# Causal mask of the scores: two VectorE additions in the accumulators in place of four TensorE products per pair of heads

## The chip, the cores and the metric

One core of a Trainium2 chip runs the whole program. The metric is the device time of one execution in microseconds (us); 1 us is 1000 ns. Engines are called PE (TensorE, its weight loads PEld), DVE (VectorE), ACT (ScalarE), POOL (GpSimd) and SP (SyncE, which here issues the loads of the weights).

## The reference, cut to what matters

Two stacks of layers run over 256 tokens of width 1024, all in float32. The first has two layers; the second has four, each made of a feed-forward part, a mixer and another feed-forward part. The four mixers are stick-breaking, block ("moba"), latent ("mla") and again stick-breaking attention, with 16 heads each. The change touches the block and the latent mixer. For 256 tokens there is one block, so block attention is plain causal attention:

```python
l_own = jnp.einsum('bhqd,bhkd->bhqk', qc, k_own).astype(jnp.float32) * scale
l_own = jnp.where(opos[None, :] <= cpos[:, None], l_own, NEG)
p = jax.nn.softmax(jnp.concatenate([l_sel, l_own], axis=-1), axis=-1)
...
logits = jnp.where(kpos[None, :] <= qpos[:, None], logits, NEG)   # latent attention
p = jax.nn.softmax(logits, axis=-1).astype(v.dtype)
```

NEG is -1e30.

## The kernel before, in words

Nearly all time goes into products with weights, which come from memory as a stream of chunks of 128 x 2048 float32 (a ring of 6). Each chunk is split in two parts: ScalarE writes the high part (`split_hi`, L204), VectorE the rest (`split_lo`, L211), in rings of 3, and TensorE makes three products of each pair of tiles (high x high, high x low, low x high). `chunk_used` tells that a chunk's parts may be overwritten.

Each engine runs one instruction stream in order, written out by hand, and the streams meet only through semaphores (`sig` names an event, `when` waits for it). There is no planner at run time; the order of the work between the attention's operations is fixed by the tables `PLAN` (block) and `LAT_STEPS` (latent): each step p of the loop over the 8 pairs of heads has three parts of other work ("feed": products of the projections that later pairs need, and early products of the output projection).

The accumulator memory has two tensors of four banks, `acc` and `tb`. Banks 0 and 1 of `tb` take the scores of the two heads of a pair: columns 0 to 127 are queries 0 to 127 against keys 0 to 127, columns 128 to 383 are queries 128 to 255 against all keys. So the parts that need a triangular mask are columns 0 to 127 and 256 to 383. Banks 2 and 3 take the transposed probabilities.

In step p, with the line numbers of the profile:

- TensorE (`softmax_pe`): waits for the exponentials of pair p-1 (`exps`), because the scores overwrite the banks that ScalarE read; makes the scores, L1161 (128 x 128) and L1163 (128 x 256), two of each; adds the mask with four products of the bf16 identity and the bf16 mask (L1166, L1167) and signals `scores`. In block attention L1161 and L1163 use 64 rows of the array, in latent attention 128. Then it waits for `weights` of pair p-1 and transposes them (L1177), runs two parts of feed, multiplies the transposed probabilities with the values (L870, L873, `heads_out`), and runs the third part of feed.
- VectorE (`softmax_dve`): waits for `scores`; takes the maximum over the columns, L1224 (128 x 256) and L1225 (128 x 512), scales it, L1227, and signals `top`; does its feed of part 0; waits for `exps`; takes the reciprocal of the sums, L1231, multiplies the probabilities, L1234 and L1235, and signals `weights`; does its feed of parts 1 and 2. Its feed is the splits L211 and, in block attention, the rotation of the positions (L1086, L1087, L1089, event `turned`, which waits for TensorE's L1021), in latent attention the taking of the queries (L1540).
- ScalarE (`softmax_act`): copies the transposed probabilities of pair p-1 to memory (L1198 in block, L1201 in latent attention); waits for `top`; makes the exponentials, L1207 and L1209, two of each with a row that reads the sum, and signals `exps`; then its feed: in block attention the copy L1071 (event `copied`, for which TensorE's rotation L1021 waits) and the splits L204, in latent attention L1521, L1531 and L204.

After every second pair L879 (ScalarE) and L883 (VectorE) take the heads' output. The mask is a constant `cst[:, C_CAUSNEG:...]`, 128 x 128 float32 with -1e30 above the diagonal; at the start of the program VectorE casts it to bf16 (L2311) for L1166 and L1167.

Of the kernel before, what the change touches and what calls it, by code (L numbers as in the profile page):

```python
# [21 lines left out]
P = 128  # L22
SEQ, D = 256, 1024
# [19 lines left out]
CAUSAL = P + SEQ  # L43
# [12 lines left out]
C_ROT, C_FOLD, C_TRI, C_ALL, C_STRICT, C_CAUSNEG, C_STRNEG = [P + 1 + i * P for i in range(7)]  # L56
# [5 lines left out]
class Signals:  # L62
# [14 lines left out]
    def sig(self, name, key, by=1):  # L77
        sem = self.sem(name)
        self.count[name] += by
        assert (name, key) not in self.marks, (name, key)  # L80
        self.marks[name, key] = self.count[name]
        return sem, by

    def when(self, name, key):
        return self.sem(name), 1 if self.known is None else self.known[name, key]
# [18 lines left out]
def write(nc, known, stream, x, pT, positions, gains, gains_T, lam_qk, lru_cols, gates, consts, out):  # L104
    f32, f32r, bf16 = mybir.dt.float32, mybir.dt.float32r, mybir.dt.bfloat16
    ALU, ACT, AX = mybir.AluOpType, mybir.ActivationFunctionType, mybir.AxisListType
# [3 lines left out]
    with ctx:  # L110
        def sb(name, shape, dt=f32):
            return ctx.enter_context(nc.sbuf_tensor(name, shape, dt))

        S = Signals(known, lambda name: ctx.enter_context(nc.semaphore(name)))
        sig, when = S.sig, S.when
# [13 lines left out]
        cst = sb("cst", [P, C_END])  # L129
# [7 lines left out]
        tb = ctx.enter_context(nc.psum_tensor("tb", [P, 4, 512], f32))  # L137
# [3 lines left out]
        ident_b, causal_b, strict_b = bfc[:, 0, :], bfc[:, 1, :], bfc[:, 2, :]  # L141
# [720 lines left out]
        def heads_out(pe, i, m, v, w):  # L862

            g, at = m // 2, SEQ * (m % 2)
            if m % 2 == 0 and g >= 2:
                pe.wait_ge(*when("cat_lo", (i, g - 2)))
            o = [acc[HD * u:HD * u + HD, head_bank(g), at:at + SEQ] for u in range(2)]
            for u in range(2):
                hd = 2 * m + u
                pe.matmul(o[u], v[:, 0, hd * HD:(hd + 1) * HD], w(u)[:, 0:SEQ], start=True, stop=True)  # L870
            for u in range(2):
                hd = 2 * m + u
                last = pe.matmul(o[u][:, P:SEQ], v[:, 1, hd * HD:(hd + 1) * HD], w(u)[:, SEQ:CAUSAL], start=False,  # L873
                                 stop=True, skip_group_check=True)
            last.then_inc(*sig("head_out", (i, m)))
# [278 lines left out]
        def softmax_pe(pe, i, c_out, n, q, k, v, p_T, feed, qk_ready, v_ready):  # L1154
            for p in range(N_PAIRS + 1):
                if p < N_PAIRS:
                    qk_ready(p)
                    if p:
                        pe.wait_ge(*when("exps", (i, p - 1)))
                    for u in range(2):  # L1160
                        pe.matmul(tb[:, u, 0:P], q(2 * p + u)[:, 0:P], k(2 * p + u)[:, 0:P], start=True, stop=True)  # L1161
                    for u in range(2):
                        pe.matmul(tb[:, u, P:CAUSAL], q(2 * p + u)[:, P:SEQ], k(2 * p + u), start=False, stop=True,  # L1163
                                  skip_group_check=True)
                    for u in range(2):
                        pe.matmul(tb[:, u, 0:P], ident_b, causal_b, start=False, stop=True, skip_group_check=True)  # L1166
                        last = pe.matmul(tb[:, u, 2 * P:3 * P], ident_b, causal_b, start=False, stop=True,  # L1167
                                         skip_group_check=True)
                    last.then_inc(*sig("scores", (i, p)))
                if p >= 1:  # L1170
                    m = p - 1
                    pe.wait_ge(*when("weights", (i, m)))
                    if m:
                        pe.wait_ge(*when("flip_out", (i, m - 1)))
                    for u in range(2):
                        for j in range(3):
                            last = pe.transpose(tb[:, 2 + u, j * P:(j + 1) * P],  # L1177
                                                probs[:, 2 * (m % 2) + u, j * P:(j + 1) * P], ident)
                    last.then_inc(*sig("flipped", (i, m)))
                feed.some(p, 0)  # L1180
                feed.some(p, 1)
                if p >= 1:
                    m = p - 1
                    pe.wait_ge(*when("flip_out", (i, m)))
                    v_ready(m)
                    heads_out(pe, i, m, v, lambda u: p_T(m, u))
                feed.some(p, 2)
            out_rest(pe, i, c_out, n)
# [30 lines left out]
        def softmax_dve(dve, i, scale, behind):  # L1219
            for p in range(N_PAIRS + 1):  # L1220
                if p < N_PAIRS:
                    pair = slice(2 * p, 2 * p + 2)
                    dve.wait_ge(*when("scores", (i, p)))
                    dve.tensor_reduce(mx[:, pair, 0], tb[:, 0:2, 0:P], AX.X, ALU.max)  # L1224
                    dve.tensor_reduce(mx[:, pair, 1], tb[:, 0:2, P:CAUSAL], AX.X, ALU.max).then_inc(*sig("own", ("mx", i, p)))  # L1225
                    dve.wait_ge(*when("own", ("mx", i, p)))
                    dve.tensor_scalar(nmx[:, pair, :], mx[:, pair, :], -scale, None, ALU.mult).then_inc(*sig("top", (i, p)))  # L1227
                behind(p, 0)
                if p < N_PAIRS:
                    dve.wait_ge(*when("exps", (i, p)))  # L1230
                    dve.reciprocal(rs[:, pair, :], sm[:, pair, :]).then_inc(*sig("own", ("rs", i, p)))  # L1231
                    dve.wait_ge(*when("own", ("rs", i, p)))
                    pr = probs[:, 2 * (p % 2):2 * (p % 2) + 2, :]
                    dve.tensor_tensor(pr[:, :, 0:P], pr[:, :, 0:P], rs[:, pair, 0:1].to_broadcast([P, 2, P]), ALU.mult)  # L1234
                    dve.tensor_tensor(pr[:, :, P:CAUSAL], pr[:, :, P:CAUSAL], rs[:, pair, 1:2].to_broadcast([P, 2, SEQ]),  # L1235
                                      ALU.mult).then_inc(*sig("weights", (i, p)))
                behind(p, 1)
                behind(p, 2)
                if p >= 2 and p % 2 == 0:
                    cat_lo(dve, i, p // 2 - 1)  # L1240
# [195 lines left out]
        class LatFeed(Feed):  # L1436
# [24 lines left out]
            def q(self, unit, p):  # L1461
                pe, i = self.pe, self.i
                if p == 0:
                    pe.wait_ge(*when("q_lo", (i, 1)))
                for u in range(2):
                    o = lat_bank(unit)[:, u * SEQ:(u + 1) * SEQ]
                    for kt in range(3):
                        at_ = 3 * (2 * p + u) + kt
                        k, a = self.c + UP_Q[at_ // Q_BLOCKS], P * (at_ % Q_BLOCKS)
                        if (u, kt) == (0, 0) or at_ % Q_BLOCKS == 0:  # L1470
                            pe.wait_ge(lo_done, k + 1)
                        hi, lo = w_hi[:, k % SPLIT, a:a + P], w_lo[:, k % SPLIT, a:a + P]
                        pe.matmul(o, hi, q_T[:, kt, 0, :], start=kt == 0, stop=False)
                        pe.matmul(o, hi, q_T[:, kt, 1, :], start=False, stop=False)
                        last = pe.matmul(o, lo, q_T[:, kt, 0, :], start=False, stop=kt == 2)
                        if at_ % Q_BLOCKS == Q_BLOCKS - 1:
                            last.then_inc(chunk_used, 1)
                if p < HEADS // 2 - 1:
                    last.then_inc(*sig("pair_done", (i, p)))

            def k(self, unit, g, b):
                pe, k = self.pe, self.c + UP_KV[g]
                pe.wait_ge(lo_done, k + 1)
                if (g, b) == (0, 0):
                    pe.wait_ge(*when("kv_lo", (self.i, 1)))
                s = k % SPLIT
                for f in range(2):
                    o = lat_bank(unit)[:, f * SEQ:(f + 1) * SEQ]
                    for kt in range(2):
                        a = kt * D + (2 * b + f) * P  # L1490
                        hi, lo = w_hi[:, s, a:a + P], w_lo[:, s, a:a + P]
                        pe.matmul(o, hi, kv_T[:, kt, 0, :], start=kt == 0, stop=False)
                        pe.matmul(o, hi, kv_T[:, kt, 1, :], start=False, stop=False)
                        last = pe.matmul(o, lo, kv_T[:, kt, 0, :], start=False, stop=kt == 1)
                last.then_inc(*sig("k_done", (self.i, g, b)))
# [1005 lines left out]
```

## Time and profile before

| | |
|---|---|
| median of 3 runs | 2611.5 us (2610.76 to 2611.63) |
| the profiled execution | 2610.73 us, span 2608.9 us |
| busy: PE, PEld, DVE, ACT, POOL | 2572.1, 2228.0, 1674.5, 1380.8, 61.1 us |
| mean granted clock of TensorE | 0.998 |
| chain that ended last, by engine | PE 92%, DVE 4%, ACT 3%, issue 1% |
| L1166 and L1167 | 32 instructions each |
| L1224, L1225, L1227 | 16 instructions each |

The span runs from the first to the last instruction of the profiled execution; the time includes what lies around it. A busy share says how long an engine worked, not whether somebody waited for it. The chain of waits is followed back from the last instruction: at each step to what released it. The block attention's loop lies at about 1343 to 1430 us of the span, the latent one's at 1853 to 1910 us. The starts of matmuls are recorded and their ends are modelled, so two matmuls in a row overlap in the rows; their pace is read from the starts.

### The profile page before, as it was taken

How to read it: one execution, taken by the hardware profiler on the slowest of the kernel's cores; microseconds unless marked ns; L12 is line 12 of the kernel's file. 1: busy time of each engine (PE TensorE's matmuls, PEld its weight loads, DVE VectorE, ACT ScalarE, POOL GpSimd, SP SyncE). 2: the span in 40 equal slices, each digit the busy share in tenths (PEclk: the TensorE clock that was granted, in tenths of full speed). 3: DMA queues.
4: the chain of work that ended last, by engine and by line, in shares of the span. 5: the costliest groups of instructions: out<-in, count | busy, mean ns of one | idle time of the engine just before them, and what ended most of it. 6: DMA issues, size and time to landing. Idle time of an engine off the chain costs nothing.

```text
span 2608.9 us, 38082 instructions
## 1 busy us (share of the span) xinstructions
PE 2572.1 (99%) x14854; PEld 2228.0 (85%) x14854; DVE 1674.5 (64%) x1827; ACT 1380.8 (53%) x1640; POOL 61.1 (2%) x30
## 2 busy tenths in 40 slices
PE   8999999999999999999999999999999999999998
PEld 7888898888888988888888888888888888898887
DVE  7766687556765666666666666666766666665665
ACT  6644565445545664454455544544654454465544
POOL 0000000001000000000000000000000000000000
PEclk9999999999999999999999999999999999999999
DMA  7455534554554345555543455454345555543551
GB/s 272 144 196 191 181 138 178 193 191 173 196 192 178 130 148 191 193 177 193 193 146 117 176 192 193 178 193 177 130 154 193 185 185 186 186 161 114 194 193 65
DMA packets 63496, 454.36 MB, mean 174 GB/s; under 512 B 7088, under 2 KB 7344, under 8 KB 8992
## 3 DMA queue, kind: packets, MB, share of 16 engines
q1 hardware_dynamic: 62064, 449.15, 48.0%
q0 software_dynamic: 896, 3.05, 0.4%
q8 instruction: 78, 1.28, 0.2%
q10 hardware_dynamic: 432, 0.68, 0.1%
q14 instruction: 26, 0.21, 0.0%
HBM read 451.79 MB, written 1.05 MB: 174 GB/s over the span
## 4 chain that ended last, share of the span: by engine, by line
PE 92%; DVE 4%; ACT 3%; issue 1%; DMA 0%; ACTq 0%; DVEq 0%
PE tb L489 28%; PE tb L494 14%; PE acc L287 10%; PE acc L288 10%; PE acc L289 10%; PE acc L253 2%; PE acc L255 2%; PE acc L256 2%; PE acc L897 1%; DVE w_lo L211 1%; PE acc L489 1%; PE acc L899 1%; PE acc L898 1%; PE tb L318 1%; ACT w_hi L204 1%
## 5 line engine op out<-in xcount | busy, mean ns | idle before, releaser
L211 DVE TENSOR_TENSOR w_lo<-raw,w_hi 128x2048 fp32r<-128x2048 f32 x416 | 952.6, 2293 | 314.7 <-ACT w_hi L204 314.5
L204 ACT ACTIVATE w_hi<-raw 128x2048 fp32r<-128x2048 f32 x425 | 812.9, 1914 | 314.4 <-PE acc L289 276.5
L489 PE MATMUL tb<-xT,w_hi 128*128 128x512 f32 x3168 | 792.0, 392 | 0.0
L489 PEld LDWEIGHTS tb<-xT,w_hi 128*128 128x128 f32 x3168 | 576.3, 188 | 108.5 <-DVE big L682 0.2
L494 PEld LDWEIGHTS tb<-xT,w_lo 128*128 128x128 f32 x3168 | 432.1, 190 | 31.0
L494 PE MATMUL tb<-xT,w_lo 128*128 128x256 f32 x3168 | 441.7, 282 | 0.0
L287 PE MATMUL acc<-w_hi,cat 128*128 128x512 f32 x1024 | 402.8, 393 | 3.5 <-DVE cat L582 3.5
L288 PE MATMUL acc<-w_hi,cat 128*128 128x512 f32 x1024 | 399.9, 390 | 0.0
L289 PE MATMUL acc<-w_lo,cat 128*128 128x512 f32 x1024 | 398.7, 389 | 0.0
L287 PEld LDWEIGHTS acc<-w_hi,cat 128*128 128x128 f32 x1024 | 192.7, 188 | 42.8 <-DVE cat L582 3.9
L289 PEld LDWEIGHTS acc<-w_lo,cat 128*128 128x128 f32 x1024 | 192.3, 188 | 41.1
L288 PEld LDWEIGHTS acc<-w_hi,cat 128*128 128x128 f32 x1024 | 192.8, 188 | 34.9
L629 ACT ACTIVATE big<-tb 128x512 f32<-128x512 f32 x80 | 47.7, 596 | 263.7 <-PE tb L494 263.7
L253 PE MATMUL acc<-xT,w_hi 128*128 128x256 f32 x560 | 167.1, 298 | 1.6 <-DVE big L1089 0.8
L639 ACT ACTIVATE big<-tb 128x512 f32<-128x512 f32 x88 | 52.7, 599 | 213.2 <-PE tb L494 213.2
L255 PE MATMUL acc<-xT,w_hi 128*128 128x256 f32 x560 | 158.2, 283 | 0.0
L256 PE MATMUL acc<-xT,w_lo 128*128 128x256 f32 x560 | 158.1, 282 | 0.0
L671 DVE TENSOR_TENSOR big<-tb,big 128x512 f32<-128x512 f32 x80 | 55.3, 691 | 142.6 <-ACT big L629 142.6
L682 DVE TENSOR_TENSOR big<-tb,big 128x512 f32<-128x512 f32 x88 | 60.8, 691 | 113.7 <-ACT big L639 113.7
L253 PEld LDWEIGHTS acc<-xT,w_hi 128*128 128x128 f32 x560 | 106.9, 191 | 7.4 <-issue 3.0
L255 PEld LDWEIGHTS acc<-xT,w_hi 128*128 128x128 f32 x560 | 107.1, 191 | 2.3 <-issue 2.2
L256 PEld LDWEIGHTS acc<-xT,w_lo 128*128 128x128 f32 x560 | 107.0, 191 | 0.0
(349 smaller groups left out, 2882.7 us busy)
## 6 DMA issues: line engine op xcount, KB each, us to landing
raw<-in_stream SPq DMA_DIRECT2D x425, 1024.0 KB, 4.8
h<-in_x SPq DMA_DIRECT2D x2, 512.0 KB, 5.9
xn<-in_gates POOLq DMA_DIRECT2D x2, 512.0 KB, 8.0
gain<-in_gains POOLq DMA_DIRECT2D x2, 512.0 KB, 5.3
out<-xn SPq DMA_DIRECT2D x2, 512.0 KB, 2.9
cst<-in_consts SPq DMA_DIRECT2D x1, 832.0 KB, 12.6
raw<-in_stream ACTq DMA_DIRECT2D x1, 512.0 KB, 8.3
raw<-in_stream SPq DMA_DIRECT2D x1, 512.0 KB, 9.1
```

What stands on the lines that cost most here:

```text
L204: act.activation(w_hi[:, k % SPLIT, :], raw[:, k % RAW, :], ACT.Copy).then_inc(hi_done, 1)
L211: dve.tensor_tensor(w_lo[:, k % SPLIT, :], raw[:, k % RAW, :], w_hi[:, k % SPLIT, :], ALU.subtract).then_inc(lo_done, 1)
L253: pe.matmul(dst(f), hi, src[:, kt, 0, :], start=kt == 0 and (after is None or f == 0), stop=False, skip_group_check=after is not None)
L255: pe.matmul(dst(f), hi, src[:, kt, 1, :], start=False, stop=False, skip_group_check=after is not None)
L256: last = pe.matmul(dst(f), lo, src[:, kt, 0, :], start=False, stop=kt == kts - 1, skip_group_check=after is not None)
L287: pe.matmul(dst(t, nn), a_hi, b_hi, start=start and kt == 0, stop=False)
L288: pe.matmul(dst(t, nn), a_lo, b_hi, start=False, stop=False)
L289: last = pe.matmul(dst(t, nn), a_hi, b_lo, start=False, stop=stop and kt == kts - 1)
L489: return pe.matmul(bank, w_hi[:, c % SPLIT, at:at + P], xT[:, kt, :, :].rearrange("p a t -> p (a t)"), start=first, stop=last)
L494: return pe.matmul(bank[:, 0:SEQ], w_lo[:, c % SPLIT, at:at + P], xT[:, kt, 0, :], start=False, stop=last)
L671: dve.tensor_tensor(two(f_sum), up_part(k or None, 0, 0), two(f_bg), ALU.add).then_inc(hid_p, 1)
L682: dve.tensor_tensor(two(f_up), up_part(k, 1, 0), two(f_bu), ALU.add).then_inc(hid_v, 1)
```

## The change

TensorE no longer adds the mask: the four products per step are gone, and `scores` is signalled by the second L1163. VectorE adds the float32 constant instead, in place in the accumulators, once for columns 0 to 127 and once for columns 256 to 383 of both heads (128 x 256 elements each), and waits for the second addition before the maxima. Nothing else is changed: the casts of the constants at the start stay.

```diff
@@ softmax_pe
                     for u in range(2):
-                        pe.matmul(tb[:, u, P:CAUSAL], q(2 * p + u)[:, P:SEQ], k(2 * p + u), start=False, stop=True,
-                                  skip_group_check=True)
-                    for u in range(2):
-                        pe.matmul(tb[:, u, 0:P], ident_b, causal_b, start=False, stop=True, skip_group_check=True)
-                        last = pe.matmul(tb[:, u, 2 * P:3 * P], ident_b, causal_b, start=False, stop=True,
+                        last = pe.matmul(tb[:, u, P:CAUSAL], q(2 * p + u)[:, P:SEQ], k(2 * p + u), start=False, stop=True,
                                          skip_group_check=True)
                     last.then_inc(*sig("scores", (i, p)))
@@ softmax_dve
                     dve.wait_ge(*when("scores", (i, p)))
+                    mask = cst[:, C_CAUSNEG:C_CAUSNEG + P].unsqueeze(1).to_broadcast([P, 2, P])
+                    dve.tensor_tensor(tb[:, 0:2, 0:P], tb[:, 0:2, 0:P], mask, ALU.add).then_inc(*sig("own", ("m0", i, p)))
+                    dve.tensor_tensor(tb[:, 0:2, 2 * P:CAUSAL], tb[:, 0:2, 2 * P:CAUSAL], mask,
+                                      ALU.add).then_inc(*sig("own", ("m1", i, p)))
+                    dve.wait_ge(*when("own", ("m1", i, p)))
                     dve.tensor_reduce(mx[:, pair, 0], tb[:, 0:2, 0:P], AX.X, ALU.max)
```

## Rows read from the trace of the kernel before

**Rows 1.** Windows: length, busy us (instructions) by engine, granted clock, DMA.

```profile
0.00:20.00 20.00, 9.31 (x48) 8.56 (x49) 7.38 (x11) 9.80 (x13) 2.10 (x8) 0.91 0.92 335
1343.00:1430.00 87.00, 83.74 (x651) 71.47 (x650) 55.42 (x80) 45.85 (x98) 0.00 (x0) 1.00 0.38 134
1853.00:1910.00 57.00, 55.62 (x400) 46.70 (x400) 38.87 (x66) 34.18 (x94) 0.00 (x0) 1.00 0.36 130
```

**Rows 2.** Chain of waits, block attention: start us, us, engine and line.

```profile
1346.80 0.61 DVE small L1225
...
1393.57 0.66 PE tb L1177 x6
...
1419.13 0.81 ACT big L1198
...
1425.96 0.61 DVE small L1225
```

**Rows 3.** Chain of waits, latent attention.

```profile
1856.85 0.61 DVE small L1225
...
1864.46 0.61 DVE small L1225
```

**Rows 4.** TensorE's waits, block attention: total us, times, longest.

```profile
PE acc L1021 <- ACT big L1071: 1.5, 2, 0.8
...
PE tb L1161 <- DVE big L1089: 0.8, 1, 0.8
PE tb L1177 <- DVE xn L1235: 0.2, 1, 0.2
```

**Rows 5.** Timeline, TensorE, block step 0: start, length, instruction, idle before.

```profile
1343.35 0.38 PE L1163 MATMUL tb<-big 64*128 64x256 f32 x2
...
1343.66 0.10 PEld L1166 LDWEIGHTS tb<-bfc 128*128 128x128 bf16 x1 [0.33 <-issue]
1343.66 0.23 PE L1166 MATMUL tb<-bfc 128*128 128x128 bf16 x1
...
1343.84 0.22 PE L1167 MATMUL tb<-bfc 128*128 128x128 bf16 x1
```

**Rows 6.** VectorE's groups by form: busy us, mean ns, idle before.

```profile
L1688 DVE TENSOR_TENSOR ropeA<-tb,cst 128x256 f32<-128x256 f32 x1 | 0.4, 424 | 3.5 <-PE tb L1567 3.5
```

**Rows 7.** Timeline, VectorE, block step 0.

```profile
1349.39 0.18 DVE L1231 RECIPROCAL small<-small 128x4 f32<-128x4 f32 x1 [1.79 <-ACT xn L1209]
1349.60 0.42 DVE L1234 TENSOR_TENSOR xn<-xn,small 128x256 f32<-128x256 f32 x1
1349.94 0.68 DVE L1235 TENSOR_TENSOR xn<-xn,small 128x512 f32<-128x512 f32 x1
```

**Rows 8.** TensorE's waits, latent attention.

```profile
PE tb L1161 <- DVE big L1540: 1.2, 1, 1.2
PE tb L1161 <- ACT xn L1209: 0.5, 1, 0.5
```

**Rows 9.** Timeline, latent steps 2, 4, 5 and 7.

```profile
1870.02 0.17 DVE L1227 TENSOR_SCALAR small<-small 128x4 f32<-128x4 f32 x1
1870.39 0.37 ACT L1207 ACTIVATE xn<-tb,small 128x128 f32<-128x128 f32 x1
...
1887.22 0.21 ACT L1209 ACTIVATION_READ_ACCUMULATOR xn<-tb,small 128x1 f32 x1
...
1887.58 0.68 PE L1161 MATMUL tb<-big 128*128 128x128 f32 x4
...
1893.18 0.21 ACT L1209 ACTIVATION_READ_ACCUMULATOR xn<-tb,small 128x1 f32 x1
...
1893.73 0.71 PE L1161 MATMUL tb<-big 128*128 128x128 f32 x4
...
1905.42 0.68 DVE L1235 TENSOR_TENSOR xn<-xn,small 128x512 f32<-128x512 f32 x1
...
1906.48 0.82 PE L1177 MATMUL tb<-cst,xn 128*128 128x128 f32 x6
```

## The prediction

> **What bounds the kernel now.** Over the whole run TensorE is busy nearly all the time, so a change that takes work from it looks like a gain. The question is what holds in the two stretches that the diff touches, the attention of block kind (1343 to 1430 us) and the latent one (1853 to 1910 us), each of 8 steps (pairs 0 to 7). First read the busy time there: TensorE 83.74 of 87.00 us and 55.62 of 57.00 us, VectorE 55.42 and 38.87 us [rows 1]. By shares TensorE is full and VectorE has a third free. Shares say nothing about order, so next comes the chain of waits. In the block stretch it does not stay on TensorE: it passes through the score maximum L1225 on VectorE in steps 0, 1, 2, 3, 5 and 7 (six such rows, the first and the last shown), and only in steps 4 and 6 through TensorE and the copy L1198 [rows 2]. In the latent stretch it passes L1225 in steps 0 and 1 and then is TensorE's [rows 3]. What closes the loop is this: maximum, then the exponentials on ScalarE, then on the same in-order ScalarE the copy L1071 and the split L204, then VectorE's split L211 and turn L1086 to L1089, and behind them in VectorE's queue the maximum of the next step. TensorE's waits show the same: it waits twice for L1071 (1.5 us), once for L1089 (0.8 us) and at the end for the weights L1235 [rows 4]. So a delay put ahead of the maximum is not swallowed by VectorE's idle third; it travels round this loop, once per step.
>
> **What is removed.** Per step four bf16 products (L1166, L1167). They start at 1343.66 us, the last at 1343.84 us, so 0.06 us apart: 4 x 0.055 = 0.22 us of TensorE per step, 3.5 us for 16 steps [rows 5]. In front of them stands an idle 0.33 us put down to "issue" [rows 5]. It would make the saving 0.5 us per step if the mask caused it; I count nothing of it, since the product ahead of them, L1163, uses 64 rows of the array and the next one 128 [rows 5], and that stays so after the removal. The Trainium skill (TensorEngine Tiling, Key Properties) says that changing the tiling mode drains TensorE, which is this case; without that rule the block stretch would gain up to 8 x 0.33 = 2.6 us more. No run so far shows the mask gone, so that is open, and it is a bound. In this trace 0.22 us of TensorE helps only where TensorE sets the pace.
>
> **What is added.** Per step two additions of 128x256 in the accumulators and a wait for the second, ahead of the two maxima. No row has VectorE writing an accumulator. The nearest is L1688, the same shape and sources (accumulator and constants, written to SBUF): 424 ns [rows 6]. Two such instructions in a row start 0.34 us apart (L1234 at 1349.60, L1235 at 1349.94), and after a wait on its own result the engine goes on 0.03 us after the end (L1231 ends at 1349.57) [rows 7]. So D = 0.34 + 0.42 + 0.04 = 0.80 us per step. The low end is 0.68 us (two starts 0.34 apart, the wait free), the high end 0.92 us (no overlap at all); below zero is excluded, since nothing goes away on VectorE. I take 0.80, from the row of the same shape. The Trainium skill (VectorE: DVE Perf Modes, the TRN2 errata) has 120 + FD cycles at 0.96 GHz with an accumulator source, by estimate 0.39 us for 256 elements, and D would be 0.77. Queued behind the wait on VectorE are the maxima and then the splits; ScalarE's exponentials wait for them, and TensorE waits for those, since the scores of step p+1 overwrite the banks that they read. No DMA is added or moved, and the cast that makes the bf16 mask stays.
>
> **The sum, block stretch.** Six steps have the maximum on the chain: 6 x 0.80 = +4.8 us. In step 4 the chain is TensorE's (L1177 at 1393.57) [rows 2], the delay of 0.80 is hidden under a product that ScalarE waits for anyway, and TensorE's saving is half felt: -0.1. In step 6 VectorE stood waiting for the scores and the exponentials behind the copy L1198 of 0.81 us [rows 2]; the scores come some 0.3 us sooner and about 0.1 is taken out of the wait for the copy, so +0.4. The last link, L1177 at the weights, waits already (0.2 us) [rows 4]. Together +5.1 us. TensorE's savings in the six steps go into longer waits.
>
> **The sum, latent stretch.** Steps 0 and 1 are on the chain: TensorE waits already 0.5 us for the exponentials [rows 8], so +1.6 us when step 2 begins. Then VectorE and ScalarE have slack, and it is used up: each step makes them later by 0.8 less what they used to wait for TensorE (in step 2 the maxima were ready at 1870.02 + 0.17 and the exponentials began at 1870.39, 0.2 us; 0.1 to 0.3 us in these steps) [rows 9], so 2.1 after step 2, 2.7 after step 3, 3.5 after step 4, while TensorE, 0.22 sooner each step, is late by only 0.9. The exponentials of step 4 end at 1887.22 + 0.21 = 1887.43 and TensorE's next scores start at 1887.58 [rows 9]: with 0.1 us between them TensorE takes over nearly all, +3.5. Step 5: exponentials late by 4.3, they ended 1893.39, the scores start at 1893.73 [rows 9], 0.3 us of slack: +4.0. In step 7 the mask starts when the scores come, so the weights L1235 are late by 4.0 - 0.2 + 0.8 = 4.6; they ended at 1906.10 and L1177 started at 1906.48 [rows 9], slack 0.4: +4.2 us. Behind it nothing waits for anything that isn't late by the same.
>
> Together 5.1 + 4.2 = +9.3 us. The profiled execution took 2610.73 us and becomes 2620.0; the median of the runs, 2611.5, lies 0.8 above it, so I forecast 2620.8. Counted as above, 15 of the 16 steps carry D in full, so D of 0.68 gives +7.5 and of 0.92 gives +11.1 (9.3 less and plus 15 x 0.12); the slacks and the savings may be off by 2 us together. The forecast's own range is 2616.7 to 2625.
>
> **Rivals.** First, no loss, the other side: at the gate where TensorE waits for L1071 and for the exponentials, the loop through VectorE and ScalarE has slack that the chain does not show, and TensorE sets the pace. Then 3.5 us are saved, 2608.0. For it speak the 83.74 of 87.00 us [rows 1]; against it the six L1225 on the chain. It decides at D: hidden if the slack per step were over 0.80 us, and 0.1 and 0.3 us are what the rows give [rows 9]. Chance 0.06. Second, half: in the latent stretch ScalarE and VectorE make up their delay and only the block stretch pays: 5.1 - 8 x 0.22 = +3.3, 2614.8; for it, the chain there is TensorE's after step 1. Chance 0.07. Third, faster: the 0.33 us in front of L1166 goes too and TensorE sets the pace, 16 x 0.55 = 8.8, 2602.7; chance 0.01. Fourth, the clock: granted clock is 1.00 in both stretches [rows 1], the longest wait of TensorE in them is 1.2 us [rows 8], and I forecast one of about 2.6 us in latent step 4. In the first 20 us, with longer pauses, it was 0.91, which is 3.6 us at 1.2 GHz, costing 1.8 us of work [rows 1]. One or two such stretches would give 2622.6 or 2624.4. The Trainium skill (TensorE: Matmul & The Clock Gate, Part 1) has the clock halved after an idle stretch of TensorE. Chance 0.05, and it lies within the range. The last 0.81 is the forecast.
>
> **The numbers.** A measurement of this kernel can tell about 0.2% (5.2 us) from no change, so slower is over 2616.7. Slower: 0.81 + 0.05 = 0.86, less 0.02 for a forecast that falls short; same: 0.06 + 0.07 + 0.02 = 0.15; faster 0.01. The range reaches down to 2614.5, into the second rival, and up to 2625.5 for a large D or the clock.
>
> **What would show it.** Two new VectorE groups of 16, each 0.42 us; L1225 to start about 0.8 us further behind the scores. Waits of TensorE for L1071 four or more times instead of two, and over 6 us; in the latent stretch waits of L1161 for L1209 of some 5 us instead of 0.5. Busy time of TensorE down by some 3 us and the span up by 9. If the block stretch is not longer by about 5 us and the latent one by about 4, the sum is wrong; if the additions last under 0.3 us or over 0.6, D is; if the total is unchanged, the loop is not what bounds.

## The result and the profile after

The changed kernel takes 2622.19 us (median of 5 runs, 2621.85 to 2623.84), the kernel before 2611.02 us beside it: a ratio of 1.0042, 95% interval 1.0031 to 1.0053, 11.2 us slower. Forecast were 2620.8 us and a range of 2614.5 to 2625.5. Measured again beside each other (e12), the same two kernels gave 2622.63 and 2612.06 us, a ratio of 1.0040 (1.0027 to 1.0054).

The page of the changed kernel hardly differs from the one before. Busy time and the chain by engine:

```profile
PE 2571.3 (98%) x14790; PEld 2226.9 (85%) x14790; DVE 1686.4 (64%) x1859; ACT 1380.2 (53%) x1640; POOL 61.1 (2%) x30
...
PE 90%; DVE 5%; ACT 3%; issue 1%; DMA 0%; ACTq 0%; DVEq 0%
```

TensorE has 64 products fewer but only 0.8 us less of busy time (their modelled lengths overlap their neighbours, and a fall of the clock, below, lengthened others), VectorE has 11.9 us more. Neither says where the 11 us are. The groups of VectorE by form do say what was added (busy us, mean ns, idle before):

```profile
L1221 DVE TENSOR_TENSOR tb<-tb,cst 128x256 f32<-128x256 f32 x16 | 6.8, 425 | 1.3 <-PE tb L1163 1.2
L1225 DVE TENSOR_REDUCE small<-tb 128x2 f32<-128x256 f32 x16 | 6.8, 424 | 0.5
L1222 DVE TENSOR_TENSOR tb<-tb,cst 128x256 f32<-128x256 f32 x16 | 6.7, 422 | 0.0
```

L1221 and L1222 are the additions, 425 and 422 ns beside the 424 ns of [rows 6]: adding in place in the accumulators takes as long as the addition of that row, which writes to SBUF. Timeline of VectorE in block step 0:

```profile
1347.02 0.42 DVE L1221 TENSOR_TENSOR tb<-tb,cst 128x256 f32<-128x256 f32 x1
1347.35 0.42 DVE L1222 TENSOR_TENSOR tb<-tb,cst 128x256 f32<-128x256 f32 x1
1347.80 0.42 DVE L1225 TENSOR_REDUCE small<-tb 128x2 f32<-128x256 f32 x1
```

From the first addition to the first maximum it is 0.78 us, forecast 0.80. TensorE's waits (total us, times, longest), first in the block stretch (1342 to 1450 us), then in the latent one (1855 to 1920 us):

```profile
PE acc L1021 <- ACT big L1071: 7.3, 4, 2.0
PE tb L1173 <- DVE xn L1236: 1.7, 1, 1.7
PE tb L1161 <- DVE big L1089: 0.8, 1, 0.8
```

```profile
PE tb L1161 <- ACT xn L1205: 5.1, 4, 2.7
PE tb L1161 <- DVE big L1541: 1.2, 1, 1.2
PE tb L1173 <- DVE xn L1236: 0.3, 1, 0.3
```

The wait for the copy L1071 went from 1.5 us in two places [rows 4] to 7.3 us in four (6.3 us in e7, whose clock does not fall), the one for the weights of the last pair (L1173 on L1236, before L1177 on L1235) from 0.2 us to 1.7, the one for the exponentials (L1205 is L1209 of before) from 0.5 [rows 8] to 5.1 us. That is where the time is. In the chain of waits of the latent stretch the second maximum now appears seven times, where it appeared twice [rows 3]:

```profile
1864.73 0.61 DVE small L1226
...
1873.14 0.61 DVE small L1226
...
1878.70 0.61 DVE small L1226
...
1885.29 0.61 DVE small L1226
...
1895.40 0.61 DVE small L1226
...
1902.14 0.61 DVE small L1226
...
1913.55 0.61 DVE small L1226
```

**The same in lengths.** The two stretches can be cut out of any profile: from the start of the first L1161 of the attention to the start of the next L318 (the transposes for the next layer). They repeat within 0.1 us between profiles as long as the clock stays, far closer than the totals, which drift by 1 to 2 us between executions. "Falls" counts how often the granted clock went to half in the stretch.

```
profile                      block (falls)  latent (falls)
before                       101.20 (0)     64.78 (0)
changed                      107.79 (1)     68.97 (0)
changed again (e12)          108.81 (2)     69.03 (0)
e1 splits held, VectorE      101.54 (0)     65.23 (0)
e2 splits held, TensorE       99.60 (0)     63.87 (0)
e3 changed, filled waits     106.24 (0)     69.43 (1)
e4 one addition              108.36 (2)     68.54 (0)
e5 no mask                   100.82 (0)     63.80 (0)
e6 mask by both              106.63 (0)     70.19 (1)
e7 block alone changed       106.21 (0)     64.76 (0)
e8 latent alone changed      101.17 (0)     69.38 (1)
e9 additions twice           115.70 (2)     75.09 (1)
e10 e2, one split more        98.92 (0)     63.86 (0)
e11 mixed                     98.38 (0)     63.15 (0)
```

Step by step, the delay of the scores of pair p (start of its first L1161, changed less before, each stretch counted from its own pair 0):

```
pair      1     2     3     4     5     6     7
block   0.79  1.59  1.40  3.68  3.51  5.43  5.24
latent  0.57  1.59  1.35  1.12  3.42  4.02  3.92
```

Call a gate a place where TensorE waits for L1071 or for the exponentials. At each gate it takes over all that VectorE and ScalarE are late (0.79, 1.59, then 3.2); between the gates it gains back 0.2 us per step, the removed products. The 3.68 at block pair 4 and the 5.43 at pair 6 hold a part that the additions do not explain, the fall of the clock: in e7, without a fall, they are 3.16 and 3.84. Busy time and granted clock by the microsecond around it (the column behind the five engines is the clock):

```profile
1387.00:1388.00 1.00, 0.00 (x0) 0.00 (x0) 0.00 (x0) 1.00 (x5) 0.00 (x0) 1.00 0.00 0
1388.00:1389.00 1.00, 0.99 (x3) 0.58 (x3) 0.00 (x0) 1.00 (x1) 0.00 (x0) 0.80 0.00 0
1389.00:1390.00 1.00, 1.00 (x5) 0.67 (x4) 0.22 (x1) 0.75 (x1) 0.00 (x0) 0.50 0.00 0
...
1391.00:1392.00 1.00, 1.00 (x7) 1.00 (x6) 1.00 (x2) 0.00 (x0) 0.00 (x0) 0.50 0.00 0
1392.00:1393.00 1.00, 1.00 (x9) 0.82 (x10) 0.97 (x4) 0.00 (x0) 0.00 (x0) 1.00 0.00 0
```

```profile
1388.01 1.53 PE L1021 MATMUL acc<-big,cst 128*128 128x512 f32 x2 [1.93 <-ACT big L1071]
...
1390.19 0.41 PE L998 MATMUL acc<-w_hi,xT 128*128 128x256 f32 x1
1390.40 0.41 PE L999 MATMUL acc<-w_lo,xT 128*128 128x256 f32 x1
```

TensorE stood idle for 1.93 us (timeline, second fence), and from about 1388.6 to 1392 us it ran at 1.2 GHz: a product every 0.21 us instead of every 0.12. Without a fall the stretch is 106.2 us (e3 and e7), so the fall cost 1.55 us.

### The profile page after: what moved, and what is told of

Same layout as the page of the kernel before. It is cut to its first block, busy times and chain, and to the rows that moved or that the text cites. A ratio compares the mean times of both kernels' runs of the same rounds, so it can differ in the third digit from the quotient of the medians.

```text
span 2620.0 us, 37986 instructions
## 1 busy us (share of the span) xinstructions
PE 2571.3 (98%) x14790; PEld 2226.9 (85%) x14790; DVE 1686.4 (64%) x1859; ACT 1380.2 (53%) x1640; POOL 61.1 (2%) x30
## 3 DMA queue, kind: packets, MB, share of 16 engines
HBM read 451.79 MB, written 1.05 MB: 173 GB/s over the span
## 4 chain that ended last, share of the span: by engine, by line
PE 90%; DVE 5%; ACT 3%; issue 1%; DMA 0%; ACTq 0%; DVEq 0%
PE tb L489 27%; PE tb L494 14%; PE acc L287 10%; PE acc L288 10%; PE acc L289 10%; PE acc L253 2%; PE acc L255 2%; PE acc L256 2%; DVE w_lo L211 1%; PE acc L897 1%; PE acc L489 1%; PE tb L318 1%; PE acc L899 1%; PE acc L898 1%; PE acc L997 1%
## 5 line engine op out<-in xcount | busy, mean ns | idle before, releaser
L211 DVE TENSOR_TENSOR w_lo<-raw,w_hi 128x2048 fp32r<-128x2048 f32 x416 | 952.5, 2292 | 315.3 <-ACT w_hi L204 315.1
```

Source lines behind the costliest of these rows:

```text
L211: dve.tensor_tensor(w_lo[:, k % SPLIT, :], raw[:, k % RAW, :], w_hi[:, k % SPLIT, :], ALU.subtract).then_inc(lo_done, 1)
```

## The experiments

Theory: the additions lie on a loop through VectorE's and ScalarE's in-order queues that had almost no slack, so their 0.8 us is paid in nearly every step. Rivals: the additions cost time by themselves (VectorE in the accumulators); or TensorE's products set the pace; or the clock makes the difference.

### Each half of the change (e5, e6), each stage (e7, e8)

**e5** takes the four products out of the kernel before and puts nothing in their place; it leaves out the causal mask of both mixers:

```diff
-                        pe.matmul(tb[:, u, 0:P], ident_b, causal_b, start=False, stop=True, skip_group_check=True)
-                        last = pe.matmul(tb[:, u, 2 * P:3 * P], ident_b, causal_b, start=False, stop=True,
```

> The kernel before without the four mask products and without any mask: leaves out the causal mask of block and latent attention. Loop theory: TensorE's 0.22 us per step count only where TensorE sets the pace, block steps 4 and 6 and latent steps 2 to 7, so 1.8 us less than before (2609.2), the removed 0.33 us in front of L1166 reappears in front of the next product. Rival, TensorE sets the pace everywhere: 3.5 us less (2607.5); with the 0.33 us gone too, 6 to 8.8 us less.

Measured 2611.15 against 2612.45 us, ratio 0.9996 (0.9987 to 1.0005): 1.3 us less. The interval of the total reaches from 3.4 us less to 1.3 more and decides little. The lengths do: block 0.38 us shorter, latent 0.98, together 1.4 us, near the 1.8 of the loop theory and far from the 3.5 that the products occupy. And the idle 0.33 us is still there, now in front of the next product (timeline of the weight loads):

```profile
1343.28 0.31 PEld L1163 LDWEIGHTS tb<-big 64*128 64x128 f32 x4
1343.92 0.19 PEld L253 LDWEIGHTS acc<-xT,w_hi 128*128 128x128 f32 x1 [0.33 <-issue]
```

In the kernel before it stood in front of L1166 in the 8 block steps (L1166's idle time "issue: 2.7, 8") and in none of the 8 latent ones, where L1163 uses 128 rows as well. So it belongs to the step from 64 to 128 rows of the array, not to the mask; the Trainium skill's sentence on tiling modes (TensorEngine Tiling, Key Properties) agrees.

**e6** leaves the products in and puts the additions behind them.

> Mask added twice, by TensorE's products and by VectorE's additions (the sum of both masks the same entries out). Loop theory: the whole cost of the changed kernel and about 1 us more, the saving of TensorE's products being felt in some five steps: 2622 to 2624. Rival, the removal is worth its full 3.5 us: 2625.7.

Measured 2621.92 against 2612.45 us, ratio 1.0038 (1.0024 to 1.0052): 9.5 us, not the 11 or 12 that I had expected. In its profile the block stretch has no fall of the clock; whether that holds for the other four executions is not known. The block stretch is 106.63 us, only 0.4 us longer than with the products gone (106.24, e3). In the latent stretch it is 70.19 us, 1.2 over the changed kernel, and a fall of the clock is mixed in; with some 0.4 us for it, as in e8, an estimate of 0.8 us is left for the products. So almost all of the cost is the additions', and the removal gives back about 1.2 us of it.

**e7 and e8** make the change under `if i == 1` (block) or `if i == 2` (latent) alone.

> The change in block attention alone, latent attention as before. Loop theory: +5.1 us, and +1.5 where the clock falls, so 2616 to 2618. Rival (only the stretch with TensorE's own waits pays): the whole 11 us here.

> The change in latent attention alone, block attention as before. Loop theory: +4.2 us, 2615.2, with TensorE waiting 5 us for the exponentials; perhaps 1.5 us more where the clock falls behind the idle 2.7 us of step 4. Rival (slack of VectorE and ScalarE there swallows it): under +1 us.

Measured 2618.39 and 2616.98 against 2612.45 us: ratios 1.0023 (1.0014 to 1.0032) and 1.0019 (1.0009 to 1.0028). The stretch that was changed is 5.0 us longer in e7 and 4.6 in e8 (with a fall of about 0.4 us; 4.2 in the changed kernel), the other is as before to 0.03 us. The two costs add up and do not touch each other. In both profiles the clock also fell once at 441 us, in a feed-forward stage that the change does not touch. TensorE waits there 1.8 us for VectorE's L582 (e7's waits; 1.7 us in the kernel before, whose clock stayed up), so the place is not made by the change. In e10, with the mask on TensorE throughout, the clock falls at 131 us. Falls are not the change's alone.

### The length of the additions (e4, e9)

**e4** makes one addition of 128x512 over both parts; **e9** makes the pair twice.

```diff
-                    mask = cst[:, C_CAUSNEG:C_CAUSNEG + P].unsqueeze(1).to_broadcast([P, 2, P])
-                    dve.tensor_tensor(tb[:, 0:2, 0:P], tb[:, 0:2, 0:P], mask, ALU.add).then_inc(*sig("own", ("m0", i, p)))
-                    dve.tensor_tensor(tb[:, 0:2, 2 * P:CAUSAL], tb[:, 0:2, 2 * P:CAUSAL], mask,
-                                      ALU.add).then_inc(*sig("own", ("m1", i, p)))
+                    mask = cst[:, C_CAUSNEG:C_CAUSNEG + P].unsqueeze(1).unsqueeze(1).to_broadcast([P, 2, 2, P])
+                    own_ = tb[:, 0:2, 0:CAUSAL].rearrange("p u (b k) -> p u b k", k=P)[:, :, 0:3:2, :]
+                    dve.tensor_tensor(own_, own_, mask, ALU.add).then_inc(*sig("own", ("m1", i, p)))
```

> The changed kernel with one addition of 128x512 over both masked parts in place of two of 128x256. Loop theory: D goes from 0.80 to 0.69 + 0.04 = 0.73 us, 15 steps carry it in full, so 1.0 us less than the changed kernel (2621.2), within 0.3. Rival, a fixed cost per addition of more than the 0.08 us seen: over 2 us less.

> The changed kernel with the two additions and their wait made twice per step (the mask added twice, the same entries out). Loop theory: D goes from 0.80 to 1.60 us and every slack is used up already, so 15 to 16 steps carry 0.80 more: 12 to 13 us over the changed kernel, 6 to 6.5 of it in the block stretch (first scores to the transposes behind it, without falls of the clock 112.4 us instead of 106.2) and 5.6 to 6.4 in the latent one (74.8 instead of 69.0). Rival, part of the 9.2 us is not carried by the length of the additions (a one-time effect of VectorE writing the accumulators): less than 10 us more.

e4: 2622.77 against 2612.62 us, 1.0038 (1.0024 to 1.0051), in its total not to be told from the changed kernel, where 1.0 us less was forecast. The addition lasts 693 ns. The latent stretch is 0.43 us shorter for 7 steps of 0.06 us less, so the rival of a large fixed cost per addition is out; in the block stretch the clock fell twice. e9: 2638.48 against 2612.06 us, 1.0104 (1.0088 to 1.0119). The latent stretch is 6.1 us longer than the changed kernel's, with a fall; the block one is 9.5 us over the 106.2 without falls, and of these some 2.6 are its two falls, by estimate (e12 has two as well and is 2.6 us over 106.2, but one of e9's lies elsewhere, at the very end of the stretch). That leaves about 6.9 and 5.7 to 6.1 us for 8 steps of 0.8 each: the cost goes with the length of what stands on the loop. The total is 15.9 us over the changed kernel where 12 to 13 were forecast; three falls in the profiled execution, of which the changed kernel has one or two, account for a part.

### Slack put into the loop (e1, e2, e10)

In the order of before, VectorE's last work ahead of a maximum is often a split L211 of 2.3 us for a chunk that TensorE needs only much later. Here these splits are put in a list and issued behind the next maximum (main lines; the one of block step 6 stays where it was):

```diff
+                if part == 0:
+                    while hold:
+                        split_lo(dve, c, hold.pop(0))
...
-                        split_lo(dve, c, unit[1] + SPLIT)
+                        if hold is None:
+                            split_lo(dve, c, unit[1] + SPLIT)
+                        else:
+                            hold.append(unit[1] + SPLIT)
```

> The kernel before (mask on TensorE) with the same splits held back. Loop theory: it loses the 3.3 us of waits that TensorE has in the block stretch and 0.5 us in the latent one, so 2607 to 2609, and the additions' version in the same order is up to 3.5 us (16 x 0.22) faster than this, not slower. Rival, TensorE's products alone set the time: same as before, 2611.

> The changed kernel, with the splits L211 that stood between VectorE's feed and the next maximum held back until after that maximum (block and latent steps). Loop theory: the 0.80 us per step were paid because VectorE's queue (split, turn, maximum) and ScalarE's formed a loop with no slack; with some 2.3 us of slack per step the two additions are hidden, TensorE's waits for L1071 and for the exponentials nearly vanish, and the time is some 3 to 6 us below the kernel before (2605 to 2608). Rival, the additions cost by themselves (accumulators shared with TensorE, or the handshake): the time stays 9 us or more above the same order with the mask on TensorE.

e2 (mask on TensorE): 2609.62 against 2612.62 us, 0.9989 (0.9980 to 0.9998). e1 (mask on VectorE): 2612.77 against 2612.62, 1.0002 (0.9993 to 1.0011), where 2605 to 2608 was forecast. In this order the additions cost 1.94 us in the block stretch and 1.36 in the latent one, 3.3 us where they cost 9.2 before. The rival that they cost by themselves is out, since the same instructions cost a third when only the order around them is different. But my expectation that they would be hidden entirely was wrong. TensorE's waits in e1's block stretch:

```profile
PE tb L1177 <- DVE xn L1240: 1.7, 1, 1.7
PE acc L1021 <- ACT big L1071: 1.4, 2, 1.1
PE acc L253 <- DVE big L1089: 0.8, 1, 0.8
PE tb L1165 <- DVE big L1089: 0.7, 1, 0.7
PE acc L253 <- DVE w_lo L211: 0.6, 1, 0.6
```

and in e2's:

```profile
PE acc L253 <- DVE big L1089: 0.8, 1, 0.8
PE tb L1181 <- DVE xn L1239: 0.5, 1, 0.5
PE acc L1021 <- ACT big L1071: 0.5, 1, 0.5
PE tb L1165 <- DVE big L1089: 0.3, 1, 0.3
```

The weights of the last pair are waited for 1.7 us instead of 0.5: TensorE is through with the feed of step 7 before they come. Comparing the two profiles pair by pair, TensorE comes later with the mask on VectorE in block steps 0, 1, 3, 5 and 7 and latent steps 0, 5 and 7, and 0.2 us sooner in block 2, 4 and 6 and latent 1 to 4. **e10** is e2 with the split of block step 6 held back too.

> Mask on TensorE, splits held back as in e2, and also the split of block step 6, which stood ahead of the maximum of step 7. Loop theory: TensorE's wait of 0.5 us for the last weights goes, block stretch 99.1 us instead of 99.6, latent 63.9, 0.5 us less than e2. Rival, the split then delays the weights of step 7 by its own 2.3 us: block stretch 100 or more.

2608.84 against 2612.06 us, 0.9988 (0.9979 to 0.9997); block stretch 98.92 us, the wait of 0.5 us gone.

### A mix of both (e11)

```diff
+        BY_VECTOR = {(1, 2), (1, 4), (1, 6), (2, 1), (2, 2), (2, 3)}
```

The pairs (mixer, step) in this set take the mask by VectorE, the others by TensorE, on top of e10.

> As e10, with the mask on VectorE in the steps where e1 showed TensorE not later but 0.2 us sooner (block steps 2, 4, 6, latent steps 1, 2, 3) and on TensorE in the other ten. Loop theory: the additions are hidden there and each step gives 0.2 us: block stretch 0.5 to 0.6 us and latent 0.5 to 0.6 us shorter than e10, the shortest of all. Rival, any delay of VectorE travels on whatever the slack: longer than e10.

2607.69 against 2612.06 us, 0.9983 (0.9974 to 0.9992): faster than the kernel before by 4.4 us, and the stretches 98.38 and 63.15 us are the shortest of all, 0.54 and 0.71 below e10. Its waits in the block stretch are e10's to the digit, so the six pairs of additions are hidden. Between e10 and e11 the total's intervals overlap; the lengths tell them apart.

### The clock (e3, e12)

**e3** is the changed kernel with 16 products by a tile of zeros, added to a sum already under way, ahead of the wait for L1071 in block steps 0, 1, 3 and 5. The zeros take the place of the bf16 mask, so the first two layers' differential attention runs without its causal mask.

```diff
+                if e in (3, 4, 7, 10):
+                    for _ in range(16):
+                        self.pe.matmul(fed_bank(e + 1)[:, 0:P], causal_b, ident_b, start=False, stop=False,
+                                       skip_group_check=True)
```

> The changed kernel, with 16 products by a tile of zeros (0.055 us each, 0.9 us) ahead of four waits for L1071 in the block steps 0, 1, 3 and 5, where TensorE stands idle anyway. Clock theory: 1.5 of the 11 us come from one fall of the granted clock to 0.50 behind the idle 1.93 us of step 3; with 1.0 us of idle left the clock stays at 1.00 in the block stretch and the time is 1 to 2 us below the changed kernel (2620.5). Rival, the fall comes by itself whatever TensorE does, or the idle time is not free: same as the changed kernel (2622) or above.

> The changed kernel again beside the others on the same chip. Loop theory: block stretch 106.2 us plus 1.5 for each fall of the clock in it, latent 69.0 plus up to 0.5 for a fall; total 9 to 12 us over before, the profiled time explained by the count of falls. Rival, the falls belong to the block step 3 wait as such: one there again.

e3: 2621.94 against 2612.62 us, 1.0036 (1.0022 to 1.0050). In the block stretch the clock stays at 1.00 and the length is 106.24 us: the filling costs nothing (e7, without it, has 106.21), and no fall comes. Its waits there:

```profile
PE acc L1025 <- ACT big L1075: 2.7, 3, 1.0
PE tb L1177 <- DVE xn L1240: 1.7, 1, 1.7
```

But in its profile the clock fell in the latent stretch, which isn't filled, and once at 130 us, and the total did not come out 1 to 2 us lower: 9.3 us over before where the changed kernel has 10.6 to 11.2, which the intervals do not separate. e12, the changed kernel once more: 2622.63 against 2612.06 us. This time the clock fell twice in the block stretch, behind the waits of steps 0 and 3 (windows around both):

```profile
1349.50:1353.00 3.50, 2.10 (x4) 1.07 (x5) 1.53 (x4) 3.15 (x7) 0.00 (x0) 0.73 0.48 199
1387.00:1391.00 4.00, 2.45 (x6) 1.42 (x7) 0.68 (x1) 3.29 (x8) 0.00 (x0) 0.71 0.00 0
```

The two cost 2.6 us, less than twice 1.55, and the next wait for L1071, at step 1, is 1.05 us instead of 1.7: it took a part of the first fall's delay. The length of the wait alone does not decide whether the clock falls: there is no fall at step 3 in e7, which has the same wait of 1.9 us, and none in the changed kernel behind the 2.65 us at latent step 4, where e3, e6 and e8 have one. That filling the waits prevents falls is consistent with e3's block stretch; with one profile it is not shown, since e6 and e7 have none there either.

## Why the prediction was right

- **What bounds the stretches.** The chain's passing through L1225 was read as a loop with no slack. Shown: e7 and e8 give the cost where it was forecast, e1 and e2 take two thirds of it away with order alone, and e9, with twice the additions, costs about as much more as they are longer. One row was misread: TensorE waited for L1089 twice in the block stretch, not once; the second wait (view of the kernel before) stayed 0.8 us in e7 and e8, so the sum did not suffer:

```profile
PE acc L253 <- DVE big L1089: 0.8, 1, 0.8
```

- **D = 0.80 us.** Measured 0.78; the row of the same shape [rows 6] was the right one. The estimate from the Trainium skill (VectorE: DVE Perf Modes, the TRN2 errata), 0.39 us for each, is 8% below the 425 ns measured, which decides.
- **Block stretch +5.1 us.** Measured 106.24 - 101.20 = +5.0 without the fall. Latent stretch +4.2 us: measured 68.97 - 64.78 = +4.2. The takeover at latent pair 5 was put at 3.5 and was 3.42, with a wait of 2.65 us where about 2.6 was forecast; at pair 6 at 4.0, and was 4.02. These agreements in the single gates, and not only in the total, are what speaks against luck.
- **TensorE's saving.** 0.2 us per step between the gates, as forecast, and not more: the idle 0.33 us did not go. Removing the products alone gives 1.4 us. The third rival was priced wrongly: the pause of 0.33 us stood in front of L1166 in the 8 block steps only, so it would have given 3.5 + 2.6 = 6.1 us and not 8.8. One sign did not come: TensorE's busy time fell by 0.8 us in the whole run, not by 3. In e5, where the products are gone and the clock does not fall, the two stretches hold 3.0 us less busy time than before (159.15 for 162.12 us), in the changed kernel only 1.2 less (160.93), with the fall among them.
- **The step that failed.** The prediction gave a fall of the clock a chance of 0.05. It came in both profiles of the changed kernel, at waits of 1.9 us (both) and 1.7 us (e12), where I had looked at the one of 2.6 us. This is the larger part of 11.1 (between the profiled executions) less 9.2 us; the last 0.3 us lie outside both stretches, in stages that were not changed.
- **Not settled.** How the total's spread of 2 us divides between falls of the clock and the start and end of the program; only the profiled executions show the clock.

## What to carry to other kernels

A busy share of 64% is not slack. Before moving work to an engine, ask what stands in front of and behind the new instruction in that engine's queue, and whether the chain of waits passes through its neighbours; if it does, the work is paid once per turn of the loop, while the engine relieved gives back only what it gains between its waits. And what decides is the order: a long instruction that nobody needs soon, standing ahead of a short one that everybody waits for, was worth 3 us here without touching the work, and only where that slack exists does the moved work pay.

## What the runs showed of the hardware

- VectorE adds in place in the accumulators in 425 ns for 128x256, as long as with an output in SBUF (424 ns), and in 693 ns for 128x512; it is 0.03 us from the end of the second addition to the maximum that waits for it.
- The granted clock fell to half near the end of waits of TensorE of 1.7 to 3.6 us (from 0.3 us before the end of the wait to 1.4 us after it) in some executions and not in others of the same kernel. In the block stretch one fall cost 1.55 us and two 2.6; in the latent stretch about 0.4 us (e3, e8), and the wait of 0.5 us at the next gate is gone there.
- The idle 0.33 us in front of the first product with 128 rows behind one with 64 rows is the same with a bf16 product behind it (before) and with a float32 one (e5), and is missing where both have 128 rows (latent steps).
